# Expert layer: twelve widths of moving rows in the gate-and-up product, and one matmul for both halves up to 224 rows

## The reference

```
logits = h @ w_router + b_router;  top_val, top_idx = top_k(logits, 4);  gates = softmax(top_val)
for each expert e, over the rows (tokens) that chose it:
    hgu = rows @ w_gate_up[e] + b_gate_up[e]                  # (rows, 1024) @ (1024, 2048)
    x = min(hgu[::2], 7); y = clip(hgu[1::2], -7, 7)
    act = x * sigmoid(1.702 * x) * (y + 1)
    out[token] += gate * (act @ w_down[e] + b_down[e])        # (rows, 1024) @ (1024, 1024)
```

## Time and profile before

| | us |
|---|---|
| median of three runs | 5797.87 |
| span of the profiled execution, first to last instruction | 5798.4 |
| of it, from the first product of gates and ups to the end of the experts | 2684.5 |

### The profile page before, as it was taken

The page is one execution under the profiler, slowest core; times in us unless marked ns, Lnnn a source line. Parts: engine busy times, 40 slices in busy tenths (PEclk is TensorE's granted clock), DMA queues, the critical chain, the costliest instruction groups (busy, mean ns, idle before and its releaser), DMA issues. The chain is left out here.

```text
span 5798.4 us, 94453 instructions
## 1 busy us (share of the span) xinstructions
PE 5445.0 (94%) x31472; PEld 4862.5 (84%) x31473; DVE 3583.9 (62%) x6639; ACT 2613.8 (45%) x5152; POOL 818.5 (14%) x611
## 2 busy tenths in 40 slices
PE   8999989889799999998969999999999999999993
PEld 7777767778699999997758899999999888899893
DVE  6666757333466667776765645655656645467767
ACT  3444421333455556664334534443545434356554
POOL 1101125223000000001540101010101100010113
PEclk9999999999899999998989999999999999999997
DMA  3333244445411111102424644554656635466666
GB/s 140 116 116 106 81 143 143 133 119 143 143 59 59 50 37 39 66 9 83 159 88 145 221 130 154 194 159 156 204 176 226 223 121 170 134 217 238 235 219 226
DMA packets 260437, 809.25 MB, mean 140 GB/s; under 512 B 22304, under 2 KB 168448, under 8 KB 224512
## 3 DMA queue, kind: packets, MB, share of 16 engines
q1 hardware_dynamic: 230352, 717.05, 35.4%
q0 software_dynamic: 27536, 84.88, 6.7%
q10 hardware_dynamic: 2336, 4.45, 0.2%
HBM read 662.84 MB, written 143.47 MB: 139 GB/s over the span
## 5 line engine op out<-in xcount | busy, mean ns | idle before, releaser
L2631 ACT CAST e_wh<-r_raw 128x1024 fp32r (+1 forms) x770 | 790.2, 1042 | 1062.1 <-ACTq L2344 1060.8
L2715 DVE TENSOR_TENSOR e_wl<-r_raw,e_wh 128x1024 fp32r<-128x1024 f32 x770 | 930.1, 1222 | 520.2 <-DVEq L2344 518.9
L2564 PE MATMUL ps<-e_hT,e_wl 128*128 128x192 f32 (+4 forms) x4096 | 1219.9, 298 | 0.0
L2559 PE MATMUL ps<-e_hT,e_wh 128*128 128x256 f32 (+3 forms) x2816 | 901.2, 320 | 9.3 <-PEq L2344 9.0
L2563 PE MATMUL ps<-e_hT,e_wh 128*128 128x256 f32 (+3 forms) x2816 | 899.9, 320 | 0.0
L2564 PEld LDWEIGHTS ps<-e_hT,e_wl 128*128 128x128 f32 x4096 | 774.6, 189 | 16.2
L2559 PEld LDWEIGHTS ps<-e_hT,e_wh 128*128 128x128 f32 x2816 | 530.1, 188 | 28.8 <-issue 11.7
L2563 PEld LDWEIGHTS ps<-e_hT,e_wh 128*128 128x128 f32 x2816 | 530.2, 188 | 16.7
L2585 PE MATMUL ps<-e_wh,e_aTh 128*128 128x512 f32 x1248 | 511.9, 410 | 5.0 <-PEq L2344 4.9
L1740 PE MATMUL ps<-a_PT,a_V 128*128 128x256 f32 (+1 forms) x3264 | 502.9, 294 | 0.2 <-DVE a_PT L1825 0.2
L1785 ACT CAST a_PT<-ps 128x512 fp32r<-128x512 f32 x512 | 288.0, 589 | 464.1 <-PE ps L1725 464.1
(11 more groups left out here) (368 smaller groups left out, 9558.5 us busy)
## 6 DMA issues: line engine op xcount, KB each, us to landing
r_raw<-in_wgu SPq DMA_DIRECT2D x130, 2048.0 KB
r_raw<-in_wdn SPq DMA_DIRECT2D x64, 2048.0 KB
m_raw<-in_w SPq DMA_DIRECT2D x56, 1024.0 KB, 4.8
qTd<-p_qt SPq DMA_DIRECT2D x32, 640.0 KB, 6.6
e_bd<-in_bdn SPq DMA_DIRECT2D x32, 512.0 KB, 3.8
kTd<-p_kt SPq DMA_DIRECT2D x32, 448.0 KB, 3.7
a_Q<-qTd SPq DMA_DIRECT2D x7, 2048.0 KB, 9.0
a_V<-vd SPq DMA_DIRECT2D x24, 512.0 KB, 4.3
```

Of the source, the lines that this page charges most:

```text
L2559: t = pe.matmul(p[:, 0:v], wh, E.hT[:, 0, k, 0:v], start=(k == 0), stop=False)
L2564: t = pe.matmul(p[:, 0:v], wl, E.hT[:, 0, k, 0:v], start=False, stop=(k == 7))
L2631: act.copy(E.wh[:, h, x], raw[:, 2048 * h + 1024 * i:2048 * h + 1024 * i + 1024]).then_inc(E.hi_full, 1)
L2715: return dve.tensor_tensor(lo, src, hi.bitcast(F32), ALU.subtract)
```

## The change

The list of widths on TensorE grows from five to twelve, the one on ScalarE and VectorE from four to six, and the limit for one matmul over high and low rows goes from 192 to 224. The conditional wait for a block of rows becomes an unconditional one, since no width now covers a block that the group may lack: 128 takes groups of up to 128 rows, and 160 those of 129 to 160, which have two blocks. In the pattern of the bank the 256 columns become 224; for v up to 224 it is the same.

```diff
-WIDTHS = (192, 256, 384, 448, 512)
-TAKEN = (192, 256, 384, 512)
-BOTH = 192
+WIDTHS = (128, 160, 192, 224, 256, 288, 320, 352, 384, 416, 448, 512)
+TAKEN = (128, 160, 224, 288, 384, 512)
+BOTH = 224
...
-    def gate_up(v, blocks):
+    def gate_up(v):
         for b in range((v + 127) // 128):
-            with present(pe, blocks, b) if v < 256 else nullcontext():
-                take(pe, E.hT_full[b])
+            take(pe, E.hT_full[b])
...
-                both = p[:, :].rearrange("p (y n) -> p y n", y=2)[:, :, 0:min(v, 256)]
+                both = p[:, :].rearrange("p (y n) -> p y n", y=2)[:, :, 0:min(v, BOTH)]
...
-        by_width(pe, m, lambda v: gate_up(v, r), WIDTHS)
+        by_width(pe, m, gate_up, WIDTHS)
```

## The result

The changed kernel takes 6216.4 us (median of 4 runs, 6205.5 to 6224.1) beside 5796.9 us for the kernel before on the same chip: ratio 1.0723, 95% interval 1.071 to 1.0736. That is slower by 7.2%, where the forecast said 1.8% and its range ended at 6020. The profiled execution has a span of 6211.3 us, 412.9 more than before.

What follows compares the result with a forecast made beforehand. TensorE's pace was taken as the bound, with VectorE near it at 192 columns. 5798.4 - 91.5 (fewer columns) + 198 (code fetched again) = 5905 us, slower by 1.8%; range 5700 to 6020.

Steps and rivals of the forecast that it cites:

- 11 packets: TensorE's loop over groups: grows from 6 instruction packets to 11, about 2750 instructions, assumed not to stay beside the engine.
- the price of a landing: TensorE branch to missing code: 2.9 us with idle DMA, some 3.5 us with the loads busy here.
- the cover by the queue: Matmuls already queued on TensorE hide about 4.3 us of the 10.5 us of code fetching per group.
- the clock: Rival: refetch idle time drops TensorE to 1.2 GHz, 3 us in each group, 96 us, giving 6000; chance 0.13.
- Columns: Gate and up passes in the experts' stage: fewer streamed columns at the new widths gain 91.5 us.
- The seven narrow passes: Groups going from 192 columns to 160 or 128: gains of 8 and 7.5 us, limited by VectorE and loads.
- The 2.4 us lost: Groups of 161, 180, 172 rows: VectorE's round of 4.70 us exceeds TensorE's 4.59, costing 0.8 us each.
- The rival by which the columns don't pay: VectorE, not TensorE, bounds the passes: only wide ones give, 76 us; shifts each case by 15, no separate chance.
- The rival by which all code stays: TensorE's longer loop is never fetched again and the columns come through: 5706 us (5684 to 5722); chance 0.28.
- The rival by which the queue covers most of it: Some TensorE code is refetched, mostly under the queue's 2.85 us: 93 us cost, 5800 (5750 to 5830); chance 0.14.
- Landings: TensorE branches to missing code in tree, tree ends and down: 3 a group (2 to 4), half before the product.
- the middle of 93 and 355: Refetch cost over 32 groups taken as 198 us, between 2 landings a group (93) and 4 (355).

Runs made afterwards that it cites:

- e9: Kernel before with seven TensorE widths (192, 224, 256, 288, 352, 448, 512), five on VectorE and ScalarE, 186 idle instructions ahead of TensorE's program: 5752.9 us, ratio 0.993.
- e8: Kernel before with six TensorE widths (128, 160, 224, 256, 384, 512) and five on VectorE and ScalarE, to test the narrow ones: 5832.5 us, ratio 1.0059.
- e10: Same seven widths as e9 without the 186 idle instructions, against the kernel before: 5831.9 us, ratio 1.006.
- e1: Kernel before with seven unused copies of gate_up added on TensorE, columns unchanged: 6365.4 us, ratio 1.0987.
- e11: Changed kernel with VectorE's and ScalarE's four old widths and conditional waits for row blocks: 6238.5 us, ratio 1.0766 to the kernel before.
- e3: Kernel before with two unused copies more on VectorE and ScalarE (192 three times), TensorE unchanged: 5873.0 us, ratio 1.0132.
- e5: Kernel before with one unused copy more on TensorE (192 twice): 5800.7 us, ratio 1.0009.
- e6: e5 with 100 idle semaphore increments ahead of TensorE's program: 5928.0 us, ratio 1.0222 to the kernel before.
- e2: Kernel before with two unused copies more on TensorE (192 and 448 twice): 5889.0 us, ratio 1.0165.
- e4: Kernel before with six TensorE widths (192, 224, 256, 352, 448, 512), five on VectorE and ScalarE, 256 columns in one matmul for both halves: 5751.3 us, ratio 0.9926.
- e12: e4 with 64 idle semaphore increments ahead of VectorE's program: 5818.4 us, ratio 1.0038 to the kernel before.
- e7: e3 with 100 idle semaphore increments ahead of VectorE's program: 5912.8 us, ratio 1.0195 to the kernel before.

## Why the prediction was wrong

The direction and the mechanism were right, with the chances on its side (0.60 for slower). That 11 packets do not stay was taken without a row that shows a limit; the runs put the limit near seven. The size was wrong, and the time lies 196 us above the upper end of the range. The steps that failed are the price of a landing, the cover by the queue, and the clock, which was kept out of the sum.

**Columns: right.** 352 columns: 61.3 us for 61.2 forecast. 224: 41.3 for 41.6. 288: 51.1 in e9, for 51. 416: 73.2 for 73.0. The seven narrow passes give less than forecast: in e8 7.7 us together and not 15.5, and as much is waited for after the product. The 2.4 us lost where VectorE takes 224 columns for 192 no run isolates. In the passes alone the sum is some 84 us in place of 91.5. The rival by which the columns don't pay is right below 192 columns and wrong above.

**That code is fetched again: right.** The rival by which all code stays is out: it needed 11 packets to stay, and in e10 not even 7 packets' worth did, spread over eight. The rival by which the queue covers most of it is out too: the gaps grew by 387.5 us.

**Landings: right in number, wrong in price.** Three a group were forecast, and the 96 behind the first product are 3.0. But I priced each at 3.5 us, from the one landing of 2.9 with an idle DMA; their mean is 4.9, and the worst 8.4. This is 96 x 1.4 = 134 us, the largest term. A single row of an undisturbed fetch of one packet was raised by a guess of 20%; the measured rise is 70%. Part of it is the load (3.3 to 5.1 us for one packet), part that half of the landings wait for two packets.

**The cover: wrong.** I let 4.3 us a group lie under the matmuls already issued. The gaps between passes grew by 387.5 us against 470.5 of long branches, so 83 were covered, 2.6 a group: 55 us. The 198 was also called the middle of 93 and 355, which is 224. A landing follows another at one boundary, as at 4763.9, and the queue covers the first alone.

**The clock: right as a rival, wrong to be kept out of the sum.** I gave it 0.13 and 96 us. Passes down, which have the same matmuls as before, are 49.9 us longer, and those of gates and ups give 37.2 in place of 84: together 97 us of slower passes. Not all of it need be the clock, since VectorE fetches too; e1, where it fetches nothing, has 85 us of the same. A hole of some 6 us in every group stood in my own sum, so this cost belonged to the forecast, not beside it. That 96 comes so near to it is luck: it stood for 3 us in each of 32 groups, and was not worked out from a row.

**The entry** was not in the sum: 14.1 us.

Forecast 5905 + 97 (slower passes) + 134 (price) + 55 (cover) + 14 (entry) + 7 (columns) - 1 (end of the program) = 6211, for a span of 6211.3. The cover is what is left between the branches and the gaps, so that the sum closes proves nothing.

**What the prediction left out.** The copies on VectorE and ScalarE were never counted. In this kernel that cost little in the end (e11), but by luck: with the TensorE loop of before, which stays, it costs 78 us (e3), near all that the columns give.

## What to carry to other kernels

When a list of shapes becomes a list of copies in a loop at run time, count the loop's instructions on every engine before counting what the shapes save, and look at the instruction queues inside the loop: here the time rose in every run in which they spoke. A code fetch by a branch is not hidden by the engine's queue when several come in a row, its price rises with the load on the DMA engines and with the packets waited for (3.3 to 5.75 us on average here), and the lower clock behind each hole comes on top. Within a budget of code choose the shapes by what they save: three widths (224, 352 and 256 in one matmul for both halves) bring 46 us here; the two narrowest bring nothing once the gaps are counted (e8), and cost two copies.

## What the runs showed of the hardware

- TensorE's instructions come in blocks of 256 (16 KB): 65 packets for the 16,589 that it ran in the attention stage, 255 each. A loop that by my count touches seven blocks stays (e5, e9), one that touches eight does not (e6, e10), though the loop has the same length in either pair (1634 and 1778 instructions). This fits a store of eight blocks in which the next block in order is always fetched ahead; that reading is the simplest that fits all the runs, and it is not shown by itself. The Trainium skill, "Runtime: NRT & Kernel Launch" (Instruction fetch mechanics), gives TensorE a memory of 2048 instructions. e2's loop of 1843 and e6's of 1634 are shorter than that, and both fetch again.
- A landing on missing code costs TensorE 4.0 us with one packet and 5.75 with two (49 and 50 branches of the changed kernel); with one packet, 3.3 us under 30% DMA load and 5.1 from 60% on.
- VectorE's blocks are half as large (8 KB; 126 instructions a packet with ScalarE's in the attention stage), and its limit is much lower: 325 instructions stay in one place and not in another (e4, e12), 373 did not in both places tried (e3, e7). A fetch there shows on the queue and as a hole after the branch, not as a long branch.
- 64 to 186 idle instructions ahead of a program change its time by 1 to 2% (e5 to e6: 127 us; e10 to e9: -79 us; e4 to e12: +67 us). An edit elsewhere in the program that moves the loop could do the same, so a comparison of two kernels near this limit needs the instruction queues beside the times.
